# GpSimd's low halves in 256-column pieces, and the attention ratio as a tensor_scalar

## The chip, the cores and the metric

The program runs on one core of a Trainium2 chip. The metric is the device time of one execution in microseconds (us). The core has five engines that run side by side, each with a queue of its own: TensorE (PE; its weight loads are shown as PEld), VectorE (DVE), ScalarE (ACT), GpSimd (POOL) and SyncE (SP, which only issues transfers here). They wait for each other through semaphores.

## The reference, cut to what matters

Two transformer blocks run on 512 tokens of width 1024, all in float32. The first has a differential attention of 8 heads, a SwiGLU layer, a gated convolution and a second SwiGLU layer, with a layer norm behind each. The second has a windowed attention beside an mLSTM, a merge, and a mixture of 32 experts of which each token takes two.

```python
# first block, attention: two softmaxes per head, one subtracted from the other
p = jax.nn.softmax(s, axis=-1)
a = p[:, :, 0] - lam * p[:, :, 1]
return jnp.einsum('bhqk,bkhe->bqhe', a.astype(v.dtype), v)

def swiglu(x, w_gate, w_up, w_down):
    h = jax.nn.silu(jnp.einsum('bsd,df->bsf', x, w_gate)) * jnp.einsum('bsd,df->bsf', x, w_up)
    return jnp.einsum('bsf,fd->bsd', h, w_down)
```

## The kernel before, in words

**The split of every weight.** A float32 product is made of three products in the faster fp32r format: a = a_hi + a_lo, b = b_hi + b_lo, and a_hi b_hi + a_hi b_lo + a_lo b_hi (lines L1774 to L1776). So each weight has to be split on the core. The weights come in pairs of chunks. A pair is a tile of 128 partitions by 2 chunks by up to 512 columns, 1024 elements per partition. Four such tiles form a ring (`RING = 4`): SP loads `wraw`, ACT rounds it to `whi` (L651, semaphore `w_hi`), POOL takes `wraw - whi` into `wlo` (L1016, semaphore `w_lo`), and PE waits for `w_lo` before its first product with the pair (`pair_ready`). PE's `w_used` frees the slot. Some pairs are written to places of their own beyond the ring (`dst`: `wo_hi`, `cout_hi`, and the slots in `hhi` and `hlo`). The loops `splits` and `extra_splits` on POOL call `split` once for each pair: 224 times with 1024 columns, 32 times with 768 (the convolution's input weights, 2 by 384) and 4 times with 512 (the key and value columns, 2 by 256), 260 instructions at L1016 in all. The mixture of experts splits nothing.

**The first attention.** It runs over 32 units, `u` for a block of 128 queries and a head. For each unit DVE takes the maxima of the scores (`peak`, L1249 and L1250), ACT makes the exponentials and their sums `lsum`, and DVE's `mix` takes the reciprocals `rl` of the two sums (L1256), the ratio `lsum0 * (-lam) * rl1` (L1257) and the mixed probabilities `attn = prob1 * ratio + prob0` (L1260). PE turns `attn` (L2007), ACT copies it, PE multiplies it with the values (L2016), and DVE's `keep_o` scales the result (L1266). Each DVE instruction goes through `run`, which makes the next wait for its end. POOL splits six pairs during these units: the four first pairs of the output projection at units 4, 6, 8 and 10, two more at 12 and 14.

**The tails of the stages.** Behind each projection a norm runs tile by tile on DVE (`ln_half`, `ln_rest`: L1155, L1156, L1161, L1165, L1167, L1170; in the second SwiGLU layer also L1362), and PE turns the normed tiles (L1791). ACT and POOL meanwhile split the four first pairs of the next stage. The second block's attention has L1488 to L1490 per unit on DVE, its mLSTM L1513 and L1523 to L1536.

Of the kernel before, what the change touches and what calls it, by code (L numbers as in the profile page):

```python
# [7 lines left out]
F32 = mybir.dt.float32  # L8
# [3 lines left out]
ALU = mybir.AluOpType  # L12
# [117 lines left out]
def build(nc, A, out):  # L130
    ctx = ExitStack()
    with ctx:

        base = (nc.sbuf_base + 63) // 64 * 64
        at = [base]

        def place(name, shape, dt, where=at):
            size = int(np.prod(shape[1:])) * 4
            t = nc.alloc_sbuf_tensor_at(name, shape, dt, offset=where[0])
            where[0] += (size + 31) // 32 * 32  # L140
            return t

        def sem(name):
            return ctx.enter_context(nc.semaphore(name))


        wraw = place("wraw", [P, RING, 2, BANKF], F32)
# [17 lines left out]
        lsum = place("lsum", [P, 2, 2], F32)  # L165
# [14 lines left out]
        lams = place("lams", [P, 8], F32, aa)  # L180
# [3 lines left out]
        rl = place("rl", [P, U1, 2], F32, aa)  # L184
        ratio = place("ratio", [P, 2], F32, aa)
# [139 lines left out]
        w_lo = sem("w_lo")  # L325
# [682 lines left out]
        def _(pool):  # L1008
            lo = Count(w_lo)

            def split(cols=BANKF, dst=None):

                s = lo.mod(RING)
                pool.wait_ge(w_hi, lo.now + 1)
                h, l = dst or (whi[:, s, :, 0:cols], wlo[:, s, :, 0:cols])
                pool.tensor_tensor(l, wraw[:, s, :, 0:cols], h.bitcast(F32), ALU.subtract).then_inc(w_lo, 1)  # L1016
                lo.add()

            def extra_splits(his, los):
                for dst in zip(his, los):  # L1020
                    split(dst=dst)

            def splits(n, cols=BANKF):
                with turns(pool, n // RING, {lo: RING}):
                    for _ in range(RING):
                        split(cols)
                for _ in range(n % RING):
                    split(cols)
# [103 lines left out]
        def _(dve):  # L1132
# [5 lines left out]
            def run(ins, count=step):  # L1138

                ins.then_inc(count.sem, 1)  # L1140
                dve.wait_ge(count.sem, count.add())
# [110 lines left out]
            def mix(u):  # L1252
                nk = (u // HEADS + 1) * P
                q = u % 2
                dve.wait_ge(exp_done, 2 * u + 2)
                run(dve.reciprocal(rl[:, u, :], lsum[:, q, :]))  # L1256
                run(dve.scalar_tensor_tensor(ratio[:, q:q + 1], lsum[:, q, 0:1], lams[:, 5:6], rl[:, u, 1:2], ALU.mult, ALU.mult))  # L1257
                if u >= 2:
                    dve.wait_ge(a_turned, u - 1)
                run(dve.scalar_tensor_tensor(attn[:, q, 0:nk], prob[:, q, 1, 0:nk], ratio[:, q:q + 1],  # L1260
                                             prob[:, q, 0, 0:nk], ALU.mult, ALU.add), ar)
# [196 lines left out]
            for k in range(U1):  # L1458
                n, h = divmod(k, HEADS)
# [3 lines left out]
                q = slice(k % 2, k % 2 + 1)  # L1463
# [998 lines left out]
```

## Time and profile before

| what | value |
|---|---|
| median of 3 runs | 2208.96 us (2208.58 to 2212.13) |
| profiled execution | 2205.7 us, span 2203.8 us |
| mean granted TensorE clock | 0.967 of full speed |
| PE busy | 1986.9 us, 90% of the span |
| DVE busy | 676.3 us, 31% |
| POOL busy | 677.8 us, 31%, 382 instructions |
| ACT busy | 584.7 us, 27% |

The busy time of an engine is summed over the whole span, so a share of 31% says nothing of a stage in which that engine sets the pace. The profiled execution took 2205.7 us, 1.9 us more than its span and 3.3 us less than the median of the timed runs.

### The profile page before, as it was taken

Reading aid. Unit: us, or ns where it says so; the run is one execution under the profiler, and the core shown is the slowest. Engines: PE = TensorE matmul, PEld = TensorE weight load, DVE = VectorE, ACT = ScalarE, POOL = GpSimd, SP = SyncE. Lnnn points to the kernel's source line nnn. Section 1 sums busy time; section 2 is a strip of 40 time slices with the busy share of each in tenths; the row PEclk is TensorE's granted clock in tenths of the full one; section 3 lists DMA queues with packets and bytes.
Section 4 is the critical chain, followed back from the end, with each engine's and each line's share of the span. In section 5 each row is a group of like instructions: output and inputs, shape, how many; then the busy total and the mean of one; then the engine's idle time right before and its main releaser. Section 6 shows DMA issues by size and latency. Waiting matters only on the chain.

```text
span 2203.8 us, 29293 instructions
## 1 busy us (share of the span) xinstructions
PE 1986.9 (90%) x10761; PEld 1425.3 (65%) x10762; DVE 676.3 (31%) x1112; ACT 584.7 (27%) x984; POOL 677.8 (31%) x382
## 2 busy tenths in 40 slices
PE   8997899999999999999999999998895997777784
PEld 7874688888888878888888776765684332222221
DVE  2348641111024225111002666544637000000002
ACT  2126423333212222333322232555421000000000
POOL 4422134444434452444444342332241011011100
PEclk9997999999999999999999999999897999999997
DMA  7311023332223342333323322220156899999996
GB/s 212 113 56 50 20 87 95 95 95 96 95 77 106 96 133 75 98 95 98 101 92 100 99 87 68 74 71 15 53 199 254 361 424 427 426 427 426 422 420 241
DMA packets 155408, 362.55 MB, mean 165 GB/s; under 512 B 16671, under 2 KB 88863, under 8 KB 130752
## 3 DMA queue, kind: packets, MB, share of 16 engines
q1 hardware_dynamic: 142880, 341.35, 42.0%
q10 hardware_dynamic: 7664, 11.71, 2.0%
q0 software_dynamic: 4784, 8.40, 1.0%
q8 instruction: 52, 0.85, 0.2%
q14 instruction: 28, 0.23, 0.0%
HBM read 355.64 MB, written 14.68 MB: 168 GB/s over the span
## 4 chain that ended last, share of the span: by engine, by line
PE 69%; DMA 16%; DVE 11%; issue 2%; POOL 1%; ACT 1%; SPq 0%; POOLq 0%; DVEq 0%; ACTq 0%
PE ps L1774 20%; PE ps L1776 19%; PE ps L1775 19%; DMA wpair<-l_expert 13%; PE ps L2298 5%; DMA xg<-x2d,nowi 2%; DVE hres L1170 1%; POOL wlo L1016 1%; DVE nmax L1250 1%; PE ps L2177 1%; DVE attn L1260 1%; DVE ratio L1257 1%; DVE hres L1165 1%; PE ps L2123 1%; PE ps L2196 1%
## 5 line engine op out<-in xcount | busy, mean ns | idle before, releaser
L1016 POOL TENSOR_TENSOR wlo<-wraw,whi 128x1024 fp32r<-128x1024 f32 (+2 forms) x244 | 573.0, 2353 | 914.9 <-ACT whi L651 914.4
L1774 PE MATMUL ps<-xhi,whi 128*128 128x512 f32 (+2 forms) x1196 | 461.8, 386 | 0.9 <-POOL wlo L1016 0.7
L1776 PE MATMUL ps<-xhi,wlo 128*128 128x512 f32 (+2 forms) x1196 | 459.1, 384 | 0.0
L1775 PE MATMUL ps<-xlo,whi 128*128 128x512 f32 (+2 forms) x1196 | 459.0, 384 | 0.0
L651 ACT CAST whi<-wraw 128x1024 fp32r<-128x1024 f32 (+2 forms) x244 | 245.9, 1014 | 607.4 <-PE ps L1776 571.8
L2298 PE MATMUL ps<-wpair,mx 128*32 128x512 f32 (+1 forms) x1920 | 226.3, 618 | 68.8 <-DMA wpair<-l_expert 67.5
L1774 PEld LDWEIGHTS ps<-xhi,whi 128*128 128x128 f32 x1196 | 225.4, 188 | 45.6 <-issue 3.4
L1776 PEld LDWEIGHTS ps<-xhi,wlo 128*128 128x128 f32 x1196 | 225.2, 188 | 43.9
L1775 PEld LDWEIGHTS ps<-xlo,whi 128*128 128x128 f32 x1196 | 225.2, 188 | 42.9
L2298 PEld LDWEIGHTS ps<-wpair,mx 128*32 128x32 f32 x1920 | 69.5, 113 | 224.3 <-issue 224.1
L1324 DVE TENSOR_TENSOR scr<-scr,ps 128x1024 f32<-128x1024 f32 x22 | 26.9, 1221 | 400.1 <-ACT scr L803 400.1
L1774 PE MATMUL ps<-whi,xhi 128*128 128x512 f32 (+1 forms) x352 | 137.1, 390 | 3.8 <-DVE acol L1473 1.5
L1098 POOL COPY nowi<-idx 128x1 uint32 (+1 forms) x32 | 6.0, 188 | 422.2 <-DVE ybuf L1746 416.4
L1776 PE MATMUL ps<-whi,xlo 128*128 128x512 f32 (+1 forms) x352 | 135.1, 384 | 0.0
L1775 PE MATMUL ps<-wlo,xhi 128*128 128x512 f32 (+1 forms) x352 | 134.8, 383 | 0.0
L2298 PE MATMUL ps<-wpair,mhT 128*32 x960 | 108.6, 594 | 16.0 <-DVE mhT L1740 13.0
L1774 PE MATMUL ps<-whi,hhi 128*128 128x512 f32 x288 | 113.8, 395 | 0.0
L1776 PE MATMUL ps<-whi,hlo 128*128 128x512 f32 x288 | 113.6, 395 | 0.0
L1775 PE MATMUL ps<-wlo,hhi 128*128 128x512 f32 x288 | 113.6, 394 | 0.0
L995 ACT ACTIVATE gsil<-ps 128x512 f32<-128x512 f32 x16 | 9.6, 597 | 357.1 <-PE ps L2298 357.1
L1735 DVE TENSOR_TENSOR mh<-gsil,ps 128x512 f32<-128x512 f32 x16 | 11.0, 688 | 292.3 <-PE ps L2298 292.3
L2298 PEld LDWEIGHTS ps<-wpair,mhT 128*32 128x32 f32 x960 | 34.2, 109 | 80.5 <-issue 80.5
(383 smaller groups left out, 2354.8 us busy)
## 6 DMA issues: line engine op xcount, KB each, us to landing
wpair<-l_expert SPq DMA_DIRECT2D x180, 1024.0 KB, 26.1
wraw<-ffn_w_gate SPq DMA_DIRECT2D x88, 256.0 KB, 2.8
wraw<-ffn_w_up SPq DMA_DIRECT2D x88, 256.0 KB, 3.0
wraw<-ffn_w_down SPq DMA_DIRECT2D x44, 512.0 KB, 3.4
wraw<-w_in SPq DMA_DIRECT2D x36, 512.0 KB, 3.6
wraw<-attn_w_qkv SPq DMA_DIRECT2D x24, 512.0 KB, 9.0
wraw<-conv_w_in SPq DMA_DIRECT2D x96, 128.0 KB, 2.2
epair<-l_expert SPq DMA_DIRECT2D x12, 1024.0 KB, 17.0
```

Source lines behind the costliest of these rows:

```text
L651: act.copy(whi[:, s, :, 0:cols] if dst is None else dst, wraw[:, s, :, 0:cols]).then_inc(w_hi, 1)
L1016: pool.tensor_tensor(l, wraw[:, s, :, 0:cols], h.bitcast(F32), ALU.subtract).then_inc(w_lo, 1)
L1165: run(dve.scalar_tensor_tensor(h, h, mv[:, t, 0:1], gb[:, 0, :], ALU.subtract, ALU.mult))
L1170: run(dve.scalar_tensor_tensor(h[:, c], h[:, c], rstd[:, t:t + 1], gb[:, 1, c], ALU.mult, ALU.add), last or xn)
L1250: run(dve.tensor_reduce(nmax[:, u % 2, :], ps[:, bk:bk + 2, 0:nk], AX_X, ALU.max, negate=True), mx)
L1257: run(dve.scalar_tensor_tensor(ratio[:, q:q + 1], lsum[:, q, 0:1], lams[:, 5:6], rl[:, u, 1:2], ALU.mult, ALU.mult))
L1260: run(dve.scalar_tensor_tensor(attn[:, q, 0:nk], prob[:, q, 1, 0:nk], ratio[:, q:q + 1], prob[:, q, 0, 0:nk], ALU.mult, ALU.add), ar)
L1324: lambda g, par: dve.tensor_tensor(scr[:, 1, :], scr[:, 0, :], ps[:, 4 * par + 2:4 * par + 4, :].rearrange("p b n -> p (b n)"), ALU.mult),
L1774: pe.matmul(dst, ahi, bhi, start=start, stop=False)
L1775: pe.matmul(dst, ahi, blo, start=False, stop=False)
L1776: return pe.matmul(dst, alo, bhi, start=False, stop=stop)
L2298: mm = pe.matmul(ps[rows, bank, :], stat[:, k, rows], w, start=(k == 0), stop=(k == chunks - 1))
```

## The change

POOL's subtraction of a pair is written as several instructions: one for each of the two chunks `a`, and, where the columns of a chunk are a multiple of 256, one for each half of them. So 1024 elements per partition are done in four instructions of 256, 512 in four of 128, and 768 in two of 384. Only the last of them raises `w_lo`. The ratio of the first attention is computed by a tensor_scalar instruction, with `lsum0` as its one tensor and two columns of one element per partition as scalars, in place of a scalar_tensor_tensor with two tensors and one column.

```diff
@@ split(), on GpSimd
                 h, l = dst or (whi[:, s, :, 0:cols], wlo[:, s, :, 0:cols])
-                pool.tensor_tensor(l, wraw[:, s, :, 0:cols], h.bitcast(F32), ALU.subtract).then_inc(w_lo, 1)
+                part = cols // 2 if cols % 256 == 0 else cols
+                for a in range(2):
+                    for c in range(0, cols, part):
+                        at = slice(c, c + part)
+                        op = pool.tensor_tensor(l[:, a, at], wraw[:, s, a, at], h[:, a, at].bitcast(F32), ALU.subtract)
+                op.then_inc(w_lo, 1)
                 lo.add()
@@ mix(), on VectorE
                 run(dve.reciprocal(rl[:, u, :], lsum[:, q, :]))
-                run(dve.scalar_tensor_tensor(ratio[:, q:q + 1], lsum[:, q, 0:1], lams[:, 5:6], rl[:, u, 1:2], ALU.mult, ALU.mult))
+                run(dve.tensor_scalar(ratio[:, q:q + 1], lsum[:, q, 0:1], lams[:, 5:6], rl[:, u, 1:2], ALU.mult, ALU.mult))
```

## Rows read from the trace of the kernel before

**Rows 1.** The page, chain of work that ended last: share of the span.

```profile
PE 69%; DMA 16%; DVE 11%; issue 2%; POOL 1%; ACT 1%; SPq 0%; POOLq 0%; DVEq 0%; ACTq 0%
```

**Rows 2.** Windows view, the first attention: busy us (x instructions), granted clock, DMA share, GB/s.

```profile
154.00:246.00 92.00, 69.49 (x360) 44.44 (x360) 79.83 (x182) 61.28 (x216) 15.87 (x8) 0.80 0.11 35
```

**Rows 3.** Groups by shape, the ratio: busy us, mean ns | idle before.

```profile
L1257 DVE SCALAR_TENSOR_TENSOR ratio<-lsum,lams,rl 128x1 f32<-128x1 f32 x32 | 15.4, 481 | 1.1
```

**Rows 4.** Timeline, one unit of attention: start us, us, engine, line [idle before <-releaser].

```profile
160.25 2.34 POOL L1016 TENSOR_TENSOR wlo<-wraw,whi 128x1024 fp32r<-128x1024 f32 x1 [25.70 <-ACT whi L651]
...
160.97 1.64 DVE L1257 SCALAR_TENSOR_TENSOR ratio<-lsum,lams,rl 128x1 f32<-128x1 f32 x1
...
162.64 0.35 DVE L1260 SCALAR_TENSOR_TENSOR attn<-prob,ratio 128x128 f32<-128x128 f32 x1
...
163.05 0.47 PE L2007 MATMUL ps<-ident,attn 128*128 128x128 f32 x1 [1.74 <-DVE attn L1260]
...
164.33 0.22 DVE L1257 SCALAR_TENSOR_TENSOR ratio<-lsum,lams,rl 128x1 f32<-128x1 f32 x1
```

**Rows 5.** Timeline of POOL and of DVE, 291 to 298 us.

```profile
291.78 2.42 POOL L1016 TENSOR_TENSOR wlo<-wraw,whi 128x1024 fp32r<-128x1024 f32 x1 [36.64 <-ACT whi L651]
...
294.14 2.81 POOL L1016 TENSOR_TENSOR wlo<-wraw,whi 128x1024 fp32r<-128x1024 f32 x1
...
291.98 2.76 DVE L1170 SCALAR_TENSOR_TENSOR hres<-hres,rstd,gb 128x512 f32<-128x512 f32 x1
...
294.78 2.72 DVE L1170 SCALAR_TENSOR_TENSOR hres<-hres,rstd,gb 128x512 f32<-128x512 f32 x1
```

**Rows 6.** Timeline of PE, where it waits for normed tiles.

```profile
297.56 0.66 PE L1791 MATMUL ps<-ident,hres 128*128 128x128 f32 x4 [2.10 <-DVE hres L1170]
...
667.24 0.66 PE L1791 MATMUL ps<-ident,hres 128*128 128x128 f32 x4 [0.84 <-DVE hres L1170]
...
858.01 0.66 PE L1791 MATMUL ps<-ident,hres 128*128 128x128 f32 x4 [2.07 <-DVE hres L1170]
...
1230.53 0.66 PE L1791 MATMUL ps<-ident,scr 128*128 128x128 f32 x4 [0.95 <-DVE scr L1362]
```

**Rows 7.** Timeline of PE, the second block's attention; and DVE's line L1490: ns min/median/max.

```profile
1333.21 0.44 PE L2153 MATMUL ps<-ident,scr 128*128 128x128 f32 x2 [2.52 <-DVE scr L1490]
...
1441.27 0.55 PE L2153 MATMUL ps<-ident,scr 128*128 128x128 f32 x3 [2.27 <-DVE scr L1490]
...
1454.67 0.55 PE L2153 MATMUL ps<-ident,scr 128*128 128x128 f32 x3 [2.28 <-DVE scr L1490]
...
L1490 DVE TENSOR_SCALAR scr<-scr,rsum x32: 353/419/2557, 1307.7 to 1507.3; 128x256 f32<-128x256 f32 x16, 128x384 f32<-128x384 f32 x16
```

**Rows 8.** DVE's line L1523 in the mLSTM: ns min/median/max, first and last start.

```profile
L1523 DVE SCALAR_TENSOR_TENSOR ds<-nums x8: 165/166/2144, 1527.3 to 1573.5; 128x4 f32<-128x4 f32 x8
```

**Rows 9.** Timeline of POOL and of PE, where PE waits for POOL's splits.

```profile
813.35 9.42 POOL L1016 TENSOR_TENSOR wlo<-wraw,whi 128x1024 fp32r<-128x1024 f32 x4 [5.69 <-ACT whi L651]
...
815.80 0.50 PE L1774 MATMUL ps<-whi,yhi 128*128 128x512 f32 x1 [0.78 <-POOL wlo L1016]
...
1258.61 0.35 PE L1774 MATMUL ps<-whi,xhi 128*128 128x256 f32 x1 [0.53 <-POOL wlo L1016]
...
1271.09 0.47 PE L1774 MATMUL ps<-xhi,whi 128*128 128x512 f32 x1 [0.74 <-POOL wlo L1016]
```

**Rows 10.** Groups by shape, POOL's other subtractions: busy us, mean ns | idle before.

```profile
L1076 POOL TENSOR_TENSOR rwlo<-rwraw,rwhi 128x288 fp32r<-128x288 f32 x1 | 0.8, 797 | 0.0
L1057 POOL TENSOR_TENSOR gwlo<-gwraw,gwhi 128x128 fp32r<-128x128 f32 x1 | 0.5, 457 | 0.1
```

**Rows 11.** Timeline of all engines, 1308.2 to 1309 us.

```profile
1308.23 2.40 POOL L1016 TENSOR_TENSOR wlo<-wraw,whi 128x1024 fp32r<-128x1024 f32 x1 [15.16 <-ACT whi L651]
...
1308.63 0.15 DVE L1481 TENSOR_SCALAR nmax<-ds 128x1 f32<-128x1 f32 x1
...
1308.81 2.36 DVE L1434 TENSOR_TENSOR arow<-rows 4x512 f32<-4x512 f32 x1
```

## The prediction

> **What bounds the kernel now.** I read the chain that ended last first. PE carries 69% of the span, transfers 16% (the experts' weights at the end), DVE 11% and POOL 1% [rows 1]. So POOL's total time is hardly worth anything by itself; POOL matters where PE waits for it, and where it holds up DVE. DVE's 11% lies in a few stages, of which the windows view shows the first attention: DVE is busy 79.83 of 92.00 us there, PE 69.49 at a granted clock of 0.80 [rows 2]. The third view, groups by shape, shows that the ratio of one column costs 481 ns in the mean [rows 3], and the timeline says why: undisturbed it takes 0.22 us, but the one at 160.97 takes 1.64 us and ends at 162.61, when POOL's subtraction ends, at 160.25 + 2.34 = 162.59 [rows 4]. An instruction of DVE with two tensors in SBUF does not read while POOL's subtraction runs. PE waits 1.74 us at 163.05 for what comes of it [rows 4]. The same happens in the norms [rows 5], and I then looked for PE's waits that end with such a DVE instruction: four in tails [rows 6], three in the second block's attention [rows 7], and the start of the mLSTM's chains [rows 8]. The other way round, PE waits for POOL itself at a few places [rows 9].
>
> **What a piece costs.** The trace has no subtraction of 256 columns. 128 columns take 0.457 us and 288 take 0.797 [rows 10]: 2.1 ns a column, so 256 come to 0.73. Four instructions of 1024 columns stand 9.42 us end to end, where four of 2.40 would be 9.60 [rows 9, 11], so neighbours overlap by some 0.05 and the pitch of a piece is 0.68. Four pieces: 2.72 against 2.34 for the undivided one at its pitch (9.42 less 0.06, by four), + 0.38 a pair. Bounds: no less than the undivided one (+0), no more than 288 columns without overlap, 4 x 0.80 = 3.19 (+0.85).
>
> **Does DVE get in between two pieces?** [Rows 5] show the handing over. POOL's second subtraction starts at 294.14, before its first has ended at 294.20, and still the DVE instruction that has waited since 291.98 ends at 294.74, and POOL's second takes 2.81 instead of 2.42. So a waiting DVE goes first when an instruction of POOL ends, and POOL then waits some 0.4 us for it. With pieces DVE waits for the rest of one piece: half a pitch, 0.34 us, at a phase that is not known, 0.7 at most.
>
> The Trainium skill has a rule that speaks against this: by GPSIMD Engine Reference, section 2.1 (Instruction dispatch), consecutive Pool instructions are no barrier between its cores, each of which goes on to the next instruction as soon as its own share is done. Then the shared reads might never be free between pieces. The handover in [rows 5] speaks for a handover even so; what the rule would give is the slower rival below.
>
> **First attention.** The 32 ratios hold 15.4 - 32 x 0.22 = 8.4 us of waits [rows 3, 4], in six units, those in which POOL splits. All six are in the chain: DVE sets this loop's pace. After the change the ratio has one tensor in SBUF. [Rows 11] show such an instruction of one column, L1481 at 1308.63, take 0.15 us while POOL's subtraction runs, and its neighbour with two tensors wait 2.36. So the ratio goes through, and the next instruction, `attn` with two tensors, waits for a piece instead. Worked for [rows 4]: it is issued near 161.23 and reads some 0.2 us later (the share of a short instruction that passes inside the wait), pieces end at 160.98, 161.66, 162.34: about 0.24 instead of 1.42. Six times 0.34 is 2.1: **-6.3 us**. The ratio's own price: 0.154 for a tensor_scalar of one column without a column scalar [rows 11]; a column adds 0.220 - 0.166 = 0.054 to a scalar_tensor_tensor [rows 4, 8]; one or two of these give 0.21 to 0.26, against 0.22. Between -0.4 and +1.3 us in 32 units; I take 0. SBUF — State Buffer of the Trainium skill, section Who interferes with whom, names tensor_scalar among the instructions that can take both read ports; by that the ratio would wait for a piece as well, some 2 us of the 6.3 back. The row at 1308.63 in [rows 11] decides against it for one column.
>
> **Tails of the norms.** Before, two halves of L1170 wait one after the other for two whole subtractions (2.76 and 2.72 us [rows 5], against 0.75 undisturbed). Each would wait at most 0.7 with pieces, so DVE gains about 3.2 us, more than the 2.10 for which PE waits. The same holds at 667, 858 and 1230 us. PE's waits go as a whole and no more: 2.10 + 0.84 + 2.07 + 0.95 [rows 6] = **-6.0**.
>
> **Second attention.** PE waits 2.52, 2.27 and 2.28 us for L1490 [rows 7]. Of these 6.0 us lie in DVE's waits (2.57 at most for L1490 against 0.35 to 0.42, so up to 2.1 each). Left over are half a pitch each, and once two, since L1488 with its two tensors stands just before L1490: 4 x 0.34 = 1.4. **-4.6**.
>
> **mLSTM.** L1523 takes 166 ns undisturbed and up to 2144 [rows 8]; four chains of this kind carry 6.9 us of waits. But here L1523, L1524, L1529 or L1531 and L1532 follow each other, all with two tensors, and POOL's four pieces meet them one by one: at 1538.5 I count 0.25 + 0.43 + 0.24 instead of 1.88, in the other three 1.5, 1.1 and 1.5 instead of 2.0, 0.9 and 2.1. Saved: 1.8, of which I take **-1.5** as on PE's path.
>
> **What gets dearer.** At 813.35 POOL starts four subtractions when PE is already there, and PE waits for each in turn (815.80 is the first [rows 9]): 4 x 0.38 = 1.5. PE also waits for the first key pair (1258.61; four pieces of 128, 1.62 against 1.24) and for the first pair behind it (1271.09): 0.38 each. **+2.3**, with bounds 0 and 5.1. Elsewhere POOL's further 85 us (224 x 0.38) are covered: a pair lasts PE 5.4 us or more in the loops, and POOL needs 2.72. Without that cover each pair would cost its 0.38. No transfer is moved; SP's next load of a slot waits for `w_lo`, 0.38 later, and a slot's load takes some 3 us of a cycle of four pairs.
>
> **Sum.** -6.3 - 6.0 - 4.6 - 1.5 + 2.3 = -16.1. Against the profiled execution, 2205.7 us, this is 2189.6. The median of the runs is 3.3 us above it; against the median, 2208.96, it is 2192.9, and that is the time that I predict. Everything to the left of the experts moves their first loads too, since they are released by PE's last stages, so the gain is kept through the transfer-bound end.
>
> **Rivals.** *The handover fails (slower).* If POOL's pieces follow each other so closely that DVE waits for the fourth, each wait grows by 0.38 instead of shrinking: six in the attention (where the ratio no longer waits, so only 0.13 more each, 0.8), seven in tails, three and four in the second block: 0.8 + 14 x 0.38 + 2.3 = +8.4, 2217.4 us. For it speaks only that pieces have no wait between them, while the pair in [rows 5] had one, already met. It decides from where two thirds of the waits behave so: 18.4 us of gain less 0.66 x 24.5 and 2.3 is nothing. Chance 0.08.
>
> *Waits in series.* As in the mLSTM, each place could meet two or more pieces; if each of the 13 waits of the other stages draws two more half pitches, 8.8 us come back: 2201.7. Against it: between two instructions with two tensors the attention has 2 us of others, and the tails have PE's wait as their limit. Chance 0.17.
>
> *Dear pieces, or the gains do not reach the end (no change).* With 0.80 a piece at every place, +2.8 and residual waits a fifth longer, 2196.5; only with PE's waits refilled by something that I do not see does it come to nothing, 2209. Chance 0.06 for the latter.
>
> *More than forecast.* The waits of PE are followed by stretches at the lower of the two clock levels, 1.2 GHz, in part of the cases (0.80 in the mean of [rows 2]). If shorter waits leave the clock up, some 5 us more go: 2188. Chance 0.14. The forecast itself, 2192.9 and 2189 to 2198 around it: 0.55.
>
> **Range.** Lowest: all waits of this kind gone (8.4 + 6.0 + 6.0 + 4) and no price for pieces, -24.4: 2184.6. On the other side the series rival, and a little dearer pieces: 2204. So 2185 to 2204; beyond lie the failed handover and no change. This kernel's measurement can tell 0.2%, 4.4 us, from no change. Faster by more: 0.55 + 0.14 + 0.17 = 0.86; within: 0.06; slower: 0.08.
>
> **What the profile after would show.** POOL's subtractions in the ring at some 0.73 us, four to a pair with 2.72 between starts of pairs in a row. L1257 as TENSOR_SCALAR at a steady 0.21 to 0.26 us; `attn` with some six rows longer by up to 0.7. L1170 at no more than 1.4 us, and PE's four waits of [rows 6] gone. L1490 at no more than 1.1. PE's waits for `wlo` after 813 us at about 1.1 each instead of 0.7. The forecast is wrong if `attn` or L1170 waits 2 us still (the handover), if pieces take over 0.8 us, or if the attention's stage shortens by less than 5 us although the waits are gone.

## The result, and the profile after

The changed kernel takes 2193.8 us (median of 4 runs, 2189.1 to 2196.4), the kernel before beside it 2208.8 (2207.3 to 2212.1): a ratio of 0.9928, 95% interval 0.9906 to 0.9949. Run again later beside other kernels it took 2193.7 us (5 runs, 2190.8 to 2195.7), ratio 0.9941, interval 0.9928 to 0.9954. Forecast were 2192.9 us and 2185 to 2204.

The page of the changed kernel, its busy times and its chain; the chain's share of DVE is 9% instead of 11% [rows 1]. POOL is busy for 121 us more (85 were forecast; time in which it is held up by DVE counts as busy), and its share of the chain has not grown:

```profile
PE 1989.2 (91%) x10761; PEld 1426.7 (65%) x10762; DVE 647.0 (29%) x1112; ACT 584.1 (27%) x984; POOL 798.8 (36%) x1098
...
PE 70%; DMA 16%; DVE 9%; issue 2%; POOL 1%; ACT 1%; SPq 0%; POOLq 0%; DVEq 0%; ACTq 0%
```

The first attention, beside [rows 2] to [rows 4]: the windows view, the ratio's group by shape, and the timeline of one unit in which POOL splits. The ratio no longer waits, but each of the 32 costs 273 ns instead of 220. The mixed probabilities behind it wait 0.12 us (0.47 instead of 0.35), and PE's wait is 0.49 us instead of 1.74. The granted clock of the window is 0.87 instead of 0.80.

```profile
154.00:246.00 92.00, 70.38 (x380) 45.77 (x380) 76.66 (x186) 64.75 (x222) 23.34 (x28) 0.87 0.11 35
```

```profile
L1262 DVE TENSOR_SCALAR ratio<-lsum,lams,rl 128x1 f32<-128x1 f32 x32 | 8.7, 273 | 1.2
```

```profile
162.36 2.83 POOL L1020 TENSOR_TENSOR wlo<-wraw,whi 128x256 fp32r<-128x256 f32 x4 [25.59 <-ACT whi L651]
...
163.13 0.27 DVE L1262 TENSOR_SCALAR ratio<-lsum,lams,rl 128x1 f32<-128x1 f32 x1
163.44 0.47 DVE L1265 SCALAR_TENSOR_TENSOR attn<-prob,ratio 128x128 f32<-128x128 f32 x1
163.97 0.48 PE L2012 MATMUL ps<-ident,attn 128*128 128x128 f32 x1 [0.49 <-DVE attn L1265]
```

The first tail, beside [rows 5, 6], timelines of DVE, POOL and PE. Five lines were added to the kernel, so two lines of the norms have new numbers: L1175 is L1170 of the kernel before (512 columns), and L1170 is its L1165 (1024 columns). The numbers are those of the changed kernel from here on, and a run's own where its rows are shown. The two halves of L1175 take 2.23 us together instead of 5.48, and PE's wait of 2.10 us is gone. But POOL's pieces take longer in sum, and the last tile meets the end of them (L1170, which takes 1.28 us undisturbed, takes 1.76); there PE has two new waits of 0.61 and 0.48 us.

```profile
289.36 2.23 DVE L1175 SCALAR_TENSOR_TENSOR hres<-hres,rstd,gb 128x512 f32<-128x512 f32 x2
...
299.16 1.76 DVE L1170 SCALAR_TENSOR_TENSOR hres<-hres,mv,gb 128x1024 f32<-128x1024 f32 x1
...
301.16 2.05 DVE L1175 SCALAR_TENSOR_TENSOR hres<-hres,rstd,gb 128x512 f32<-128x512 f32 x2
...
296.32 6.34 POOL L1020 TENSOR_TENSOR wlo<-wraw,whi 128x256 fp32r<-128x256 f32 x7
...
302.12 0.66 PE L1796 MATMUL ps<-ident,hres 128*128 128x128 f32 x4 [0.61 <-DVE hres L1175]
...
303.26 0.66 PE L1796 MATMUL ps<-ident,hres 128*128 128x128 f32 x4 [0.48 <-DVE hres L1175]
```

The fourth tail holds the surprise. L1170, issued at 1230.67 while POOL runs ten pieces in a row, takes 5.38 us. It got its turn neither at the end of the piece that ran nor at one of the next: POOL's row ended at 1227.96 + 7.00 = 1234.96, DVE's instruction 1.09 us later. It had waited 4.10 us, for the rest of the piece that ran and for six more, until POOL had no piece left to run; "until POOL's queue is empty" means that below. PE stands idle for 5.19 us there. It also waits at this place without the long wait, 2.22 us in the kernel before and 2.99 in the second profile of the changed kernel, so the long wait costs it some 2.2 us.

```profile
1230.67 5.38 DVE L1170 SCALAR_TENSOR_TENSOR hres<-hres,mv,gb 128x1024 f32<-128x1024 f32 x1
...
1227.96 7.00 POOL L1020 TENSOR_TENSOR wlo<-wraw,whi 128x256 fp32r<-128x256 f32 x10
...
1240.52 0.69 PE L1796 MATMUL ps<-ident,scr 128*128 128x128 f32 x2 [5.19 <-DVE scr L1367]
```

The same wait of PE in the kernel before, and in the second profile of the changed kernel:

```profile
1243.00 1.23 PE L1791 MATMUL ps<-ident,scr 128*128 128x128 f32 x6 [2.22 <-DVE scr L1362]
...
1235.50 0.90 PE L1796 MATMUL ps<-ident,scr 128*128 128x128 f32 x3 [2.99 <-DVE scr L1367]
```

The second block, beside [rows 7, 8]: PE's waits for the row that is L1495 now, and the shortest, median and longest of three lines of DVE. L1495 is at most 0.90 us instead of 2.56; L1528, 2.14 before, at most 0.45. In their place L1493 and L1529 wait for a piece of their own.

```profile
1329.43 0.44 PE L2158 MATMUL ps<-ident,scr 128*128 128x128 f32 x2 [1.13 <-DVE scr L1495]
...
1435.03 0.55 PE L2158 MATMUL ps<-ident,scr 128*128 128x128 f32 x3 [1.34 <-DVE scr L1495]
...
1446.81 0.55 PE L2158 MATMUL ps<-ident,scr 128*128 128x128 f32 x3 [0.67 <-DVE scr L1495]
```

```profile
L1495 DVE TENSOR_SCALAR scr<-scr,rsum x32: 352/420/904, 1306.9 to 1499.4; 128x256 f32<-128x256 f32 x16, 128x384 f32<-128x384 f32 x16
...
L1493 DVE TENSOR_TENSOR rsum<-lsum x32: 158/160/720, 1306.5 to 1499.0; 128x1 f32<-128x1 f32 x32
...
L1528 DVE SCALAR_TENSOR_TENSOR ds<-nums x8: 165/166/454, 1519.1 to 1564.1; 128x4 f32<-128x4 f32 x8
...
L1529 DVE TENSOR_TENSOR ds<-ds,enm x8: 166/375/652, 1519.3 to 1564.3; 128x4 f32<-128x4 f32 x8
```

Where PE waits for POOL, beside [rows 9]:

```profile
811.77 0.79 PE L1779 MATMUL ps<-whi,yhi 128*128 128x512 f32 x1 [1.17 <-POOL wlo L1020]
...
820.01 0.50 PE L1779 MATMUL ps<-whi,yhi 128*128 128x512 f32 x1 [1.08 <-POOL wlo L1020]
...
1257.33 0.35 PE L1779 MATMUL ps<-whi,xhi 128*128 128x256 f32 x1 [0.49 <-POOL wlo L1020]
...
1270.23 0.47 PE L1779 MATMUL ps<-xhi,whi 128*128 128x512 f32 x1 [1.16 <-POOL wlo L1020]
```

To see where the time went I took from each trace the moments at which PE releases a weight pair (the semaphore `w_used`; pairs number 18, 24, 36 and so on of 260), and subtracted those of the kernel before. The stages are named by its time, and each entry is what the stage gained (-) or lost (+), in us. The last row is the difference of the whole spans. The experiments follow in the same table.

```
stage (us)   after  again  split  ratio  halves eighths 8ths   4ths   spar-  mixed
                           only   only                  spaced spaced ing
0-125        +1.8   -0.1   +1.3   +1.9   +0.1   +1.9    +2.6   +0.3   +2.9   +0.1
125-289      -4.4   -5.5   -4.3   -1.0   -4.5   -5.2    -4.4   -4.0   -6.9   -8.0   first attention
289-333      -1.4   -1.4   -1.4   +1.6   -1.6   +3.2    -2.1   -1.6   -1.4   -1.7   tail 1
333-795      -1.1   -1.1   -1.1    0.0   -1.0   -0.5    +9.0   -1.1   -1.1   -1.1   tail 2
795-852      +2.3   +2.4   +2.3   -0.1   +0.5   +6.7   +12.4   +4.2   +0.7    0.0   behind the convolution
852-905      -1.4   -1.4   -1.4   +1.6   -1.7   +3.3    -2.1   -1.6   -1.4   -1.7   tail 3
905-1223      0.0    0.0    0.0    0.0    0.0    0.0   +10.1    0.0    0.0    0.0   second SwiGLU
1223-1311    +1.8   -0.2   +5.1   +0.2   +0.1  +12.7    +7.5   +3.3   -0.2   +0.8   tail 4, keys
1311-1488    -5.4   -5.5   -5.5   +1.3   -4.0   -7.2    -7.0   -5.3   -5.5   -5.6   second attention
1488-1578    -1.3   -4.5   -7.8   -0.5   -1.8   -5.5    -5.1   -1.0   -1.2   -3.4   mLSTM
1578-2204    -0.2   +2.4   +2.3   -0.4    0.0   +2.4    +2.0   +0.1   +0.4   +1.9
sum          -9.3  -14.9  -10.4   +4.6  -14.0  +11.6   +22.8   -6.8  -13.7  -18.6
```

From 289 to 1223 the first three columns agree to 0.1 us. The first stage, the first attention and the mLSTM differ by some us between executions, with the time for which the clock is at the lower of its two levels (1.2 GHz); so do the +1.6 of `ratio_only` in two tails, where the granted clock is 0.91 (290 to 310 us) and 0.93 (845 to 870) and 1.00 in the kernel before. In the stage of the fourth tail and the keys, `split_only` has +5.1 us without any long wait of DVE: at 1270.02 PE waits 3.77 us (1.16 in the changed kernel) for a pair whose rounding on ACT stood behind a wait of ACT for DVE (8.32 us), and 10.2 us of the stage are at 1.2 GHz instead of 3.4. The last stage, whose end is set by transfers, differs by up to 2.4 us; why was not looked into. So single profiles are compared stage by stage here, and whole times by medians.

```profile
1270.02 0.52 PE L1779 MATMUL ps<-xhi,whi 128*128 128x512 f32 x1 [3.77 <-POOL wlo L1020]
```

A second figure, the sum of DVE's waits, adds up for each DVE instruction what it took above the shortest of its line and shape (where that is over 0.05 us): 58.2 us before, 31.5 in the changed kernel, 29.3 in its second profile.

### The profile page after: what moved, and what is told of

The parts are those of the page before. It is cut to its first block, busy times and chain, and to the rows that moved or that the text cites. A ratio compares the mean times of both kernels' runs of the same rounds, so it can differ in the third digit from the quotient of the medians.

```text
span 2194.5 us, 30009 instructions
## 1 busy us (share of the span) xinstructions
PE 1989.2 (91%) x10761; PEld 1426.7 (65%) x10762; DVE 647.0 (29%) x1112; ACT 584.1 (27%) x984; POOL 798.8 (36%) x1098
## 4 chain that ended last, share of the span: by engine, by line
PE 70%; DMA 16%; DVE 9%; issue 2%; POOL 1%; ACT 1%; SPq 0%; POOLq 0%; DVEq 0%; ACTq 0%
PE ps L1779 20%; PE ps L1780 20%; PE ps L1781 20%; DMA wpair<-l_expert 13%; PE ps L2303 5%; DMA xg<-x2d,nowi 2%; POOL wlo L1020 1%; PE ps L2182 1%; DVE nmax L1255 1%; DVE attn L1265 1%; PE ps L2201 1%; PE ps L1796 1%; DVE hres L1170 1%; PE ps L2128 1%; PE ps L2139 1%
## 5 line engine op out<-in xcount | busy, mean ns | idle before, releaser
L1020 POOL TENSOR_TENSOR wlo<-wraw,whi 128x256 fp32r<-128x256 f32 (+2 forms) x912 | 686.8, 785 | 788.5 <-ACT whi L651 788.4
L1329 DVE TENSOR_TENSOR scr<-scr,ps 128x1024 f32<-128x1024 f32 x22 | 26.9, 1221 | 400.1 <-ACT scr L803 400.1
```

What stands on the lines that cost most here:

```text
L1020: op = pool.tensor_tensor(l[:, a, at], wraw[:, s, a, at], h[:, a, at].bitcast(F32), ALU.subtract)
L1329: lambda g, par: dve.tensor_tensor(scr[:, 1, :], scr[:, 0, :], ps[:, 4 * par + 2:4 * par + 4, :].rearrange("p b n -> p (b n)"), ALU.mult),
```

## The experiments

**One part alone.** `split_only` keeps the old ratio, `ratio_only` the undivided subtraction.

```diff
@@ split_only, against the changed kernel
-                run(dve.tensor_scalar(ratio[:, q:q + 1], lsum[:, q, 0:1], lams[:, 5:6], rl[:, u, 1:2], ALU.mult, ALU.mult))
+                run(dve.scalar_tensor_tensor(ratio[:, q:q + 1], lsum[:, q, 0:1], lams[:, 5:6], rl[:, u, 1:2], ALU.mult, ALU.mult))
@@ ratio_only, against the kernel before
-                run(dve.scalar_tensor_tensor(ratio[:, q:q + 1], lsum[:, q, 0:1], lams[:, 5:6], rl[:, u, 1:2], ALU.mult, ALU.mult))
+                run(dve.tensor_scalar(ratio[:, q:q + 1], lsum[:, q, 0:1], lams[:, 5:6], rl[:, u, 1:2], ALU.mult, ALU.mult))
```

> The subtraction in four instructions, the ratio left as scalar_tensor_tensor with two tensors. Theory (the waits of DVE behind an undivided subtraction are what the change removes; the ratio's new form gives nothing by itself): the ratio waits for the rest of one piece where it meets one, at most 0.7 us, and the ratio is back at 220 ns instead of 273, so the 32 units get 32 x 0.053 = 1.7 us shorter; the whole 0 to 2 us faster than the changed kernel, some 2192 us, 13 to 17 us under the kernel before. Rival (the ratio's form carries part of the attention's gain): five or six ratios wait up to a whole pair again and the run is 3 to 6 us slower than the changed kernel, 2197 to 2200.

> The ratio as tensor_scalar, the subtraction undivided. Theory: the wait of up to 1.4 us moves from the ratio to the instruction behind it, the mixed probabilities with two tensors; DVE's waits in the attention stay as they are within a few tenths, and each ratio costs 0.053 us more: 2209 to 2211 us, 0 to 2 us slower than the kernel before. Rival (the ratio's form lets DVE past POOL): the attention gets 4 us shorter or more, 2205 or less.

`split_only`: 2195.6 us, ratio 0.9958 (0.9944 to 0.9973). `ratio_only`: 2208.3 us, ratio 1.0003 (0.9990 to 1.0016). The division of the subtraction is the gain, and the new ratio alone is worth nothing. But `split_only` did not come out faster than the changed kernel, as I had expected; its median is 1.9 us slower, within the intervals. What its two lines of DVE show (shortest, median, longest) speaks against my expectation:

```profile
L1262 DVE SCALAR_TENSOR_TENSOR ratio<-lsum,lams,rl x32: 219/220/786, 140.1 to 238.4; 128x1 f32<-128x1 f32 x32
...
L1265 DVE SCALAR_TENSOR_TENSOR attn<-prob,ratio x32: 352/619/915, 140.3 to 238.7; 128x128 f32<-128x128 f32 x8, 128x256 f32<-128x256 f32 x8, 128x384 f32<-128x384 f32 x8, 128x512 f32<-128x512 f32 x8
```

The ratio with two tensors waits for one piece, lets POOL's next one in, and the mixed probabilities wait for that: 1.87 + 2.58 = 4.45 us in the six units, against 0.95 with the new ratio. So by these rows the new ratio saves 3.5 us of waits and costs 32 x 0.053 = 1.7, a net 1.8. That is worked out and not shown: in the stage of the first attention `split_only` lies 0.1 and 1.2 us behind the two profiles of the changed kernel, less than what executions differ by. In `ratio_only` the wait moves, as expected, and shrinks only by the short instructions that pass inside it (6.32 us in sum instead of 8.38). Its timeline, beside [rows 4]:

```profile
162.55 2.34 POOL L1016 TENSOR_TENSOR wlo<-wraw,whi 128x1024 fp32r<-128x1024 f32 x1 [26.06 <-ACT whi L651]
...
163.32 0.27 DVE L1257 TENSOR_SCALAR ratio<-lsum,lams,rl 128x1 f32<-128x1 f32 x1
163.63 1.41 DVE L1260 SCALAR_TENSOR_TENSOR attn<-prob,ratio 128x128 f32<-128x128 f32 x1
```

**The changed kernel again.**

> The changed kernel once more, beside the others. In its first profile one DVE instruction (L1170 at 1230.67) took 5.38 us while six pieces followed each other, and PE lost about 3 us there. If that hangs on the moment at which DVE's read meets the boundary between two pieces, to within some tens of nanoseconds, it is absent from most executions, or sits at another instruction: then no instruction of this line is over 1.5 us here and the time is 3 to 4 us under the first profile, 2190 to 2193. If it belongs to the place (the order of the instructions), it is there again at over 5 us.

2193.7 us, ratio 0.9941 (0.9928 to 0.9954). L1170 of the same tile, at 1227.77 us here, waits 0.62 us instead of 4.10; no DVE instruction waits over 0.64 us. It still takes 1.91 us where I had allowed 1.5, and the median is that of the first time, not 3 to 4 us under it (the profiled execution, 2190.8 us, is 5.6 under the first). So the place alone does not bring the long wait.

```profile
1227.77 1.91 DVE L1170 SCALAR_TENSOR_TENSOR hres<-hres,mv,gb 128x1024 f32<-128x1024 f32 x1
```

**Larger and smaller pieces.** `halves` has one piece for each chunk, `eighths` pieces of 128 columns (64 for the keys and values).

```diff
@@ halves
-                part = cols // 2 if cols % 256 == 0 else cols
+                part = cols
@@ eighths
-                part = cols // 2 if cols % 256 == 0 else cols
+                part = cols // 4 if cols % 256 == 0 else cols // 3
```

> Two instructions of 512 columns to a pair, one for each chunk, with the new ratio. Theory (a waiting DVE gets in at the end of the instruction that runs): a piece is about 1.3 us, DVE's waits are up to 1.3 us instead of 0.7 and twice the rest of a quarter on average, the pair costs about 2.5 us instead of 2.72; the waits saved are two thirds of those that quarters save: about 2198 us, 3 to 6 us slower than quarters. Rival (what counts is only that POOL offers an end at all, and the further instructions cost time elsewhere): the same as quarters or faster, 2190 to 2194.

> Eight instructions of 128 columns to a pair (six for the convolution's weights), with the new ratio. At 0.457 us a piece and a pitch of some 0.41 a pair takes 3.3 us instead of 2.7. Theory (a waiting DVE gets in when the piece that runs ends, so the waits shrink with the piece, but every POOL-paced place and each last tile pays): DVE's waits in sum fall from 31 us to 20 or less, POOL's further 0.6 us a pair cost 2.4 us behind the convolution and some 0.5 in each of two tails and at the keys: 2195 to 2198, 2 to 4 us slower than quarters. Rival (the waits are what counts): 2 us faster than quarters, 2191 to 2192.

`halves`: 2193.7 us, ratio 0.9946 (0.9932 to 0.9961), the same as quarters: the rival was right. DVE waits 41.7 us in sum instead of 29.3 to 31.5, up to 1.13 us each (below, the first tail), but the table shows what comes back: PE's old waits in the tails go as a whole too, with a new one of 0.45 us in place of two (-1.6 instead of -1.4), the stage behind the convolution loses 0.5 us instead of 2.3, and only the second attention gives 1.4 us away.

```profile
287.42 4.70 POOL L1020 TENSOR_TENSOR wlo<-wraw,whi 128x512 fp32r<-128x512 f32 x3 [37.97 <-ACT whi L651]
...
287.63 3.35 DVE L1175 SCALAR_TENSOR_TENSOR hres<-hres,rstd,gb 128x512 f32<-128x512 f32 x2
```

`eighths`: 2215.4 us, ratio 1.0030 (1.0019 to 1.0041), slower than the undivided kernel (ten runs, 2210.8 to 2218.6 us), and 17 us over the upper end of my expectation. Four DVE instructions wait until POOL's queue is empty: L1170 at 298.5 (4.12 us), 868.5 (4.01) and 1244.0 (6.61), L1347 at 808.1 (2.42), together 17.2 of DVE's 26.9 us of waits. The first tail of it:

```profile
298.52 5.41 DVE L1170 SCALAR_TENSOR_TENSOR hres<-hres,mv,gb 128x1024 f32<-128x1024 f32 x1
...
297.39 5.46 POOL L1020 TENSOR_TENSOR wlo<-wraw,whi 128x128 fp32r<-128x128 f32 x13
...
304.97 1.26 PE L1796 MATMUL ps<-ident,hres 128*128 128x128 f32 x5 [4.07 <-DVE hres L1175]
```

POOL's row ends at 302.85 and DVE's instruction 1.08 us later. The handover is therefore not a law; my slower rival was a real mechanism, rare with quarters (one of some 260 waits in the two profiles of the changed kernel and that of `split_only`; none in `sparing` below) and frequent in the tails with eighths.

**What takes DVE's turn away?** First I measured the handover by itself, in a small program: POOL runs eight pieces of 256 columns with no wait between them, and DVE issues its instruction after a delay that grows from trial to trial.

```python
pool.memset(tiny[:, 0:1], 0.0).then_inc(go, 1)
...
dve.wait_ge(go, k + 1)
dve.memset(psf[:, 0:n], 0.0).then_inc(waited, 1)
dve.wait_ge(waited, k + 1)
dve.scalar_tensor_tensor(hres[:, k % TILES, :], hres[:, k % TILES, :], mv[:, 0:1], gb[:, :], ALU.subtract, ALU.mult)
```

> A small program that computes nothing of the reference (its output is zeros) and measures the handover by itself, 330 trials. In each, POOL starts eight subtractions of 256 columns, one directly behind another, and DVE, after a delay that grows by 6 columns of a memset from trial to trial, issues one scalar_tensor_tensor of 1024 columns with two tensors in SBUF, like L1170; 240 trials so, 60 with a memset of one column of POOL between the pieces, 30 with two undivided subtractions. Theory (DVE goes in when the piece that runs ends, save when its first read meets the boundary between two pieces within some tens of nanoseconds, and then it waits until POOL's queue is empty): over the delays DVE's wait is a saw-tooth between 0 and 0.7 us, with a few trials of 3 us or more, all at one phase of the boundary. Rival A (the wait at 1230.67 was a rarity of some other kind): a saw-tooth and no such trial at all. Rival B (pieces back to back are no boundary to start with, and the earlier profiles were lucky): a large share, over 20%, wait for the eighth piece.

Two neighbouring trials of its timeline; L194 is DVE's instruction, 1.28 us undisturbed:

```profile
354.26 6.57 POOL L179 TENSOR_TENSOR wlo<-wraw,whi 128x256 fp32r<-128x256 f32 x8
354.51 0.33 DVE L192 MEMSET ps<- 128x328 f32 x1 [5.09 <-POOL tiny L172]
354.88 1.28 DVE L194 SCALAR_TENSOR_TENSOR hres<-hres,mv,gb 128x1024 f32<-128x1024 f32 x1
...
361.26 0.34 DVE L192 MEMSET ps<- 128x334 f32 x1 [5.09 <-POOL tiny L172]
361.63 1.86 DVE L194 SCALAR_TENSOR_TENSOR hres<-hres,mv,gb 128x1024 f32<-128x1024 f32 x1
```

DVE is issued some 7 ns later after POOL's start (0.63 instead of 0.62 us), and waits 0.57 us more. Over 240 trials the wait is a clean saw-tooth: 0.573 us when DVE is issued 0.055 us before a piece starts, down in step with the delay to nothing at 0.16 us before the next, and none from there to 0.062 us before. Then it is POOL that waits: its next piece takes 1.70 to 1.80 us instead of 0.72. The Trainium skill, SBUF — State Buffer, "Who interferes with whom", says that issue order decides who blocks, and that the winner of the shared ports keeps them for its whole instruction; the trace agrees. The long wait at 1230.67 does not follow from issue order: six pieces that started later went first. No trial of 240 shows a long wait, nor does one of the 60 with a memset between the pieces; the 30 against undivided subtractions wait for the rest of the one that runs, up to 1.84 us. My theory that the long wait hangs on the moment at the boundary predicted some, Rival A none.

The steps of 6 ns could have stepped over it, so a finer scan followed, with smaller pieces as well.

> The small program again (output zeros, nothing of the reference is computed), 1003 trials of DVE against a row of back-to-back subtractions of POOL: 120 with pieces of 256 columns, the delay in steps of 1 column of the memset (some 1 ns) around two boundaries, where the first scan stepped over them by 6; 442 with pieces of 128 columns in steps of 2 and the 1024-column form like L1170; 221 of 128 with a 512-column form like L1175; 110 with a memset of one column between the pieces; 110 in which each piece waits for the end of the one before. Theory (a request that meets the boundary within a few ns is lost, and DVE then waits until POOL's queue is empty; shorter pieces bring more boundaries): with 256 a wait of 3 us or more in one to ten of 120 trials, next to the step of the saw-tooth; with 128 in 1 to 10% of the trials; none where each piece waits for the one before. Rival (it takes something that the small program lacks, another engine's or a transfer's traffic, or the instruction before L1170): a clean saw-tooth in all groups.

The same saw-tooth in all 1003 trials: with pieces of 256 no wait over 0.58 us, with 128 none over 0.32, and a memset or a wait between the pieces changes only hundredths. So the moment at the boundary does not suffice by itself. The last scan gave the small program what the whole kernel has besides.

> The small program a third time (output zeros and infinities apart, nothing of the reference is computed), 1345 trials, with what the two before lacked: 221 of pieces of 128 columns with a bn_aggr of DVE just before the scalar_tensor_tensor, as L1166 stands before L1170; 221 in which ACT copies pairs between SBUF tensors all the while; 221 in which SP loads 1 MB from DRAM all the while; 442 with all three; 240 of 256 columns with all three. Theory (it takes the traffic or the predecessor that the whole kernel has for DVE to lose its turn until POOL's queue is empty): waits of over 1 us in some of the trials of at least one group, most of all in the fourth. Rival (it takes something else of the whole kernel, such as PE's work or the semaphores on POOL's own instructions): no wait over 0.6 us in any group; then the condition stays open, and what is shown is only that the waits come with overlapping pieces and not with spaced ones.

Nothing again: with the bn_aggr ahead, ACT's copies, SP's loads or all of them, no wait over 0.32 us with pieces of 128 (1105 trials) and none over 0.60 with 256 (240).

What I overlooked is when DVE asks. In the three small programs it asks while one of the first five pieces of the row runs, 2.0 us after the row's start at the latest. In the whole kernels all five long waits begin late in a row of undisturbed pieces: at the 8th piece, 5.5 us after its start (the changed kernel), and in `eighths` at the 14th, 19th, 19th and 26th, 5.8 to 10.6 us after it. The fifth DVE instruction of `eighths` that asks so late and has to wait, L1170 at 672.67, waits 0.59 us, more than a piece; none that asks earlier waits over 0.31. With quarters it takes more than a long row: of 12 such instructions in three profiles one waits long, the others 0.14 to 0.62 us. So the small programs never made the case in which the long waits stand, and their saw-tooth holds for the start of a row.

**Spaced pieces.** In the whole kernel each piece waits for the end of the one before.

```diff
                     op = pool.tensor_tensor(l[:, a, at], wraw[:, s, a, at], h[:, a, at].bitcast(F32), ALU.subtract)
+                    if i < len(pieces) - 1:
+                        op.then_inc(piece_done, 1)
+                        pool.wait_ge(piece_done, ended.add())
                 op.then_inc(w_lo, 1)
+                pool.wait_ge(w_lo, lo.now + 1)
```

> Eighths, but each piece waits for the end of the one before, so that POOL's queue has a gap of some hundredth to a tenth of a microsecond at every boundary. In eighths, four DVE instructions (L1170 at 298.5, 868.5 and 1244.0 us, L1347 at 808.1) waited 4.1, 4.0, 6.6 and 2.4 us, each until POOL's queue ran empty. Theory (the long waits come from pieces that overlap their neighbours): no DVE instruction waits over 0.6 us; the four waits, 17 us in sum, go, and 0.05 to 0.1 us more per piece come on top where PE waits for POOL: 2200 to 2210, under eighths by 5 us or more. Rival (the long waits come from POOL's share of the time): they stay, and with the further time the run is over 2216.

> The changed kernel, but each piece waits for the end of the one before. Theory: DVE's waits stay at 0.7 us at most as in two of three profiles of quarters, and the pair takes 0.2 to 0.4 us more, which shows behind the convolution (0.8 to 1.6 us) and in the last tile of the tails (0.2 each): 2195 to 2197, 1 to 3 us over the changed kernel. Rival (the overlap of neighbours costs DVE its place more often than the profiles showed): as fast as the changed kernel or faster, 2190 to 2193.

`eighths_spaced`: 2227.8 us, ratio 1.0086 (1.0070 to 1.0103). `quarters_spaced`: 2196.8, ratio 0.9946 (0.9930 to 0.9963). The long waits are gone, which was the question: DVE waits 11.4 us in sum in `eighths_spaced`, none over 0.27 us (35.5 in sum and none over 0.64 in `quarters_spaced`), and L1170 (L1176 in this kernel) never takes over 1.55 us in its 16 executions, where in `eighths` it took up to 7.89:

```profile
L1176 DVE SCALAR_TENSOR_TENSOR hres<-hres,mv,gb x16: 1283/1285/1547, 269.0 to 1260.2; 128x1024 f32<-128x1024 f32 x16
```

The tails show it in the table: +3.2 and +3.3 become -2.1 each. The whole time of `eighths_spaced` I had wrong (2200 to 2210 expected; `quarters_spaced` lies in its range), for a reason of its own: the gap is 0.08 us, a piece comes every 0.54 us instead of 0.42, a pair every 4.3 instead of 3.4, and with that POOL falls behind PE at the ends of the two SwiGLU layers, which were covered up to then (+9.0 and +10.1 us), and further behind where it set the pace already (+12.4). The prediction's "without that cover each pair would cost" is what happened there.

**Fewer pieces where POOL sets the pace.** `sparing` has quarters, but whole subtractions for the four pairs behind the convolution and the four of the keys, and the new ratio in 13 units only. `mixed` has besides that halves everywhere outside the two attentions and the mLSTM.

```diff
@@ sparing, the four pairs behind the convolution, the keys and values, the ratio
-            splits(RING)
+            splits(RING, parts=1)
...
-            splits(4, 2 * KVW)
+            splits(4, 2 * KVW, parts=1)
...
+                if 3 <= u < 16:
                     run(dve.tensor_scalar(ratio[:, q:q + 1], lsum[:, q, 0:1], lams[:, 5:6], rl[:, u, 1:2], ALU.mult, ALU.mult))
+                else:
+                    run(dve.scalar_tensor_tensor(ratio[:, q:q + 1], lsum[:, q, 0:1], lams[:, 5:6], rl[:, u, 1:2], ALU.mult, ALU.mult))
@@ mixed, besides: two parts by default, four in the attentions and the mLSTM
-            def split(cols=BANKF, dst=None, parts=4):
+            def split(cols=BANKF, dst=None, parts=2):
...
-            splits(4 * 8)
+            splits(4 * 8, parts=4)
```

> Quarters as in the changed kernel, but the four pairs behind the convolution, for which PE waits one by one, and the four key and value pairs stay whole, and the ratio is a tensor_scalar in 13 of the 32 units only (those near POOL's splits), and the old scalar_tensor_tensor in the other 19. Theory (further POOL time costs where PE waits for POOL, and the tensor_scalar costs 0.053 us a unit): 1.5 to 2.3 us back behind the convolution, 0.4 at the keys, 19 x 0.053 = 1.0 in the attention: 3 us faster than the changed kernel, 2190 to 2191. Rival (what is saved there is lost again in waits of the chains behind): within 1 us of the changed kernel, 2193 to 2194.

> As sparing, but in halves wherever the loops and the norms' tails stand, and in quarters only in the two attentions and the mLSTM, where the waits of DVE are on the path that sets the end. Theory (in the tails a half saves PE's wait as a whole too, and holds up the last tile by 0.5 us instead of 1.0, twice): another 0.5 to 1 us, 2189 to 2191. Rival (DVE's longer waits for a half reach PE in the tails): slower than sparing by 1 us or more.

`sparing`: 2193.3 us (6 runs), ratio 0.9933 (0.9917 to 0.9948), which is my rival's time and not the 2190 to 2191 of the theory. `mixed`: 2190.6 (6 runs, 2182.9 to 2194.1), ratio 0.9919 (0.9901 to 0.9938). By stages both do what they should: the convolution's stage costs 0.7 and 0.0 us instead of 2.3, the attention gains 1.4 to 3.6 us more than in the changed kernel (of which 1.0 was expected; the clock has a part). In `mixed` POOL's four subtractions and PE's waits there are those of before:

```profile
802.77 9.39 POOL L1017 TENSOR_TENSOR wlo<-wraw,whi 128x1024 fp32r<-128x1024 f32 x4 [4.97 <-ACT whi L651]
...
802.82 0.47 PE L1786 MATMUL ps<-cout_hi,yhi 128*128 128x512 f32 x1 [2.02 <-DVE ylo L1361]
...
805.22 0.50 PE L1786 MATMUL ps<-whi,yhi 128*128 128x512 f32 x1 [0.76 <-POOL wlo L1017]
```

`mixed` has the lowest median of all, faster than the kernel before beyond doubt; against the changed kernel (3 us) the intervals overlap, so that is likely and not shown. `sparing` cannot be told from the changed kernel at all.

## Why the prediction was right, step by step

**A piece and its pitch: right, the pitch a little short.** Forecast 0.73 and 0.68 us, four 2.72. In the profile a piece is 0.74 us in the median and the pitch 0.69 to 0.70 (the row of ten at 1227.96 stands 7.00 us), so four pitches are 2.78 and a pair costs 0.44 more than undivided, not 0.38.

**The handover: right as the rule, not as a law.** "A waiting DVE goes first when an instruction of POOL ends" holds in all trials of the small program (0 to 0.60 us with pieces of 256), and for all but one of DVE's waits in the three profiles with quarters. The exception cost the first profile some 2 us: +1.8 in its stage, where the second has -0.2. The prediction names a wait of 2 us at "L1170" as a sign that the handover fails; that line (L1175 now) waits 0.64 us at most, but its neighbour waited 4.10, so the sign was met in all but the name. With eighths the exceptions decide the time.

**What does not contend: right for one column.** The ratio takes 272 to 273 ns in all 32 units, also beside POOL's pieces (163.13 above). The limit to one column matters: L1495 and L1347, tensor_scalar instructions too, of 256 to 512 columns, do wait for POOL (up to 2.1 us before, and 2.42 in `eighths`).

**First attention: -6.3 forecast, -4.4 and -5.5 measured.** The waits shrank more than forecast (0.95 us left, not 2.1). The failed step is the ratio's own price, "between -0.4 and +1.3 us; I take 0": it is +0.053 us each, 1.7 us, beyond my upper bound of +1.3. I had built it from a single column's price, 0.054, and counted it once or twice on top of 0.154, which gave 0.26 at most; it is 0.273. By the rows the stage should gain 8.4 - 0.95 - 1.7 = 5.7 us. The first profile's 4.4 is under the 5 us that the prediction names as a sign of being wrong, the second's 5.5 over it; how much of the difference is the clock's is not shown. The rival that shorter waits leave the clock up came true in this stage (0.87 instead of 0.80) and brought nothing beyond the forecast; over the whole execution the granted clock is 0.966, against 0.967 before.

**Tails: -6.0 forecast, of which -5.0 in the first three; -3.9 measured there.** PE's three waits are gone, as forecast. What I left out is the last tile of two of them, for which POOL's longer work reaches further: some +1.0 and +0.9 us. `halves` gives back only 0.5 there. The fourth tail and the keys, -0.2 in sum by forecast, came to -0.2 in the second profile and +1.8 in the first, which has the long wait.

**Second attention: -4.6 forecast, -5.4 and -5.5 measured.** PE's three waits are 1.13, 1.34 and 0.67 us, which is 3.9 less than before, where I had 4.6. PE's other waits of the stage are as long as before. The remaining 1.5 us fit the clock: the stage has 3.4 us at 1.2 GHz instead of 6.8, and half of the difference is 1.7. Other runs bear it out: `halves` has 2.4 us less of waits and the same 3.4 us, and gains 4.0; `ratio_only` has the waits of before and 10.2 us, and loses 1.3. So the forecast was exceeded by a term that it did not have.

**mLSTM: -1.5 forecast, -1.3 and -4.5 measured.** The lines wait in series, as I had counted, and PE's waits in the stage fall by 1.2 us in both profiles (14.5 to 13.3). The rest of the second is the clock's: 13.7 us at 1.2 GHz, where the first profile and the kernel before have 20.5.

**What gets dearer: +2.3 forecast.** Behind the convolution +1.5 was forecast and +2.3 measured. The waits for POOL are 1.17 and 1.08 us, as forecast; in addition PE waits 2.66 us instead of 2.02 for the convolution's last `ylo` at 808.9. Elsewhere the cover held: 0.0 us in 905 to 1223. It is thinner than I wrote, though: a pair of the convolution lasts PE 4.1 us and not 5.4.

**The sum.** -16.1 forecast, -9.3 in the profile that came with the result, -14.9 in the second; the medians are 15.0 and 14.3 apart. The mechanism was right; that the median was met within 1 us is luck in part, since terms too large (first attention, tails) stand against one too small (second attention), and in the second profile the clock's 3 us in the mLSTM against 2.4 lost in the last stage, through which the gain was to be kept. Of the 7 us between forecast and first profile, the long wait has some 2, the start of the kernel 1.8 (3.4 us at 1.2 GHz, where the kernel before has none there), the first attention 1.9, the first three tails 1.1 and the place behind the convolution 0.8; the second attention gives 0.8 back.

## What stays open

Why DVE loses its turn. Shown is that it happens with pieces that overlap their neighbours (five waits: one in four profiles of quarters, `sparing` with them, and four in one of eighths), each time 5.5 us or more into a row of them, that DVE then waits until POOL's queue is empty, and that it did not happen in the two kernels whose pieces wait for the one before, two profiles only. At the start of a row the phase at the boundary, a bn_aggr ahead, ACT's copies and SP's loads do not bring it. One reading would fit: the Trainium skill, GPSIMD Engine Reference, section 2.1 (Instruction dispatch), has the cores of Pool go on to the next instruction each by itself, with no barrier; if they are out of step, their reads leave DVE no gap, and a wait for the end of each piece, or the fresh start of each trial, puts them in step again. No run here shows the cores, so this is argued and not shown. The first thing to try is the small program with DVE's instruction 5 to 10 us into a longer row; PE's work and the semaphores on POOL's own pieces were not tried in it either. How often the long wait comes with quarters is open too, with one in four profiles.

## What to carry to other kernels

Where two engines exclude each other for whole instructions, cut the long instruction of the one that is not the bottleneck: the other then waits for a piece and not for the whole. Cut only as far as the waits reach the end and only where they do (halves did as much as quarters here, eighths lost all of it), since each cut costs some 0.15 us of the engine (2.34 us a pair undivided, 2.49 in halves, 2.78 in quarters, 3.4 in eighths), and in places where it sets the pace that is paid in full. Two short instructions in a row that both need the shared resource wait for two pieces; a form of the first that does not need it (the new ratio) can pay only then, and here its gain is worked out, not measured.

## What the runs showed of the hardware

A tensor_scalar of one column with two column scalars takes 0.273 us, with two constants 0.154 [rows 11]; scalar_tensor_tensor with one 0.220. POOL's subtraction costs 0.46 us for 128 columns, 0.72 to 0.74 for 256 and 2.34 for 1024; back to back they start every 0.42 us at 128 columns and every 0.69 at 256, and with a wait for the end in between 0.12 us later. Early in a row of POOL's pieces (the small programs), DVE's instruction with two tensors goes ahead of the next piece if it is issued at least 0.06 us before that starts, and then POOL waits for the whole of it. Late in a row, 5.5 us or more after its start, it can be held until POOL's queue is empty: once in four profiles with pieces of 256 columns, four times in one with 128.
